# The first two output units of an RWKV layer as fp32 products of raw weights, most of them placed between the hops of the last chain

## The chip, the core and the metric

One core of one Trainium2 chip runs the whole program in one launch. The metric is device time in microseconds (us). Engines are named as the profile names them: PE (TensorE matmuls), PEld (its weight loads), DVE (VectorE), ACT (ScalarE), POOL (GpSimd), SP (SyncE, which issues the DMA transfers). L1564 is line 1564 of the kernel.

## What is computed

Two layers over 512 latent tokens and a prefix of 256 context tokens, width 1024. Layer 0 is grouped-query attention, layer 1 a bidirectional RWKV-7 mixer; behind each mixer stands a squared-ReLU MLP. The change is at the end of the layer 1 mixer, whose result for the latent tokens is

```python
def rwkv_out(y, r, k_dir, v, g, r_k, ln_w, ln_b, w_out):
    mean = jnp.mean(y, axis=-1, keepdims=True)
    var = jnp.mean(jnp.square(y - mean), axis=-1, keepdims=True)
    yn = ((y - mean) * lax.rsqrt(var + RWKV_GN_EPS)).reshape(B, T, H * N) * ln_w + ln_b
    rk = jnp.sum((r[None] * k_dir).reshape(2, B, T, H, N) * r_k, axis=(0, -1))[..., None]
    yn = yn + (rk * v.reshape(B, T, H, N)).reshape(B, T, H * N)
    return (yn.astype(v.dtype) * g) @ w_out

x = x + mod_x[2] * y_x
x = x + mod_x[5] * sq_relu_mlp(modulate(rms_norm(x, n2), mod_x[3], mod_x[4]), w_up, w_down)
```

`y` is the output of the scan, `g` the gate, and `@ w_out` a product of 512 x 1024 by 1024 x 1024.

## The kernel before

Activations lie transposed: partitions are 128 rows of the width, 8 row blocks k = 0 to 7, tokens run along the free axis. Large products are cut into **units** of 256 output columns. A unit is 8 row blocks by 2 tiles of 128 outputs. To keep fp32 accuracy at the fast rate each operand is split into a high part and a rest of type fp32r (weights: RAW into WH by ACT, then WL = RAW - WH by POOL or DVE; activations: AH and AL), and three products are summed: WH by AH, WL by AH, WH by AL. Two buffers s = 0, 1 alternate. Units are numbered through the program: `U_OUT1` = 56 to 59 are the four of `l1_w_out`, `U_MLP1` = 60 the first of the MLP. `pe_unit` does a whole unit with 512 tokens (48 matmuls, L393); the last two output units run in halves of 256 tokens by `pe_before_norm` (`pe_part`, L571, 48 matmuls a half), so that the norm of the first 256 tokens can begin under the second half.

The scan runs by pairs of heads (8 groups g) and directions (d), so NQ = 16 chains q. `slots` interleaves in a fixed order the preparation of chain s, the inverses of chain s-1 and the hops of chain s-2; in the last slot only chain 15 is left. A chain has 12 **hops**, one per block of 64 tokens; each is a loop between PE and DVE: AR by state (L1564), DVE RH (L1664), XIF by RH (L1576), DVE VSA (L1670), VSA by BKT (L1585), DVE state SS (L1677), next hop. From hop 4 on there is also the output: SS by AR (L1573) behind RH and VSA by MT (L1590) behind VSA. The last of these ends `y` and raises `y_done`. Then, for an odd chain, comes the group norm: PE sums over a head (L1597, L1600), gate (L1603), variance (L1606); on DVE YC copy, centring (L1690), and at the end two scalings, the gate and the write of the gated rows: tokens 0 to 255 to `X[:, g, 0:256]`, 256 to 511 to `OG[:, g]` (L1707, L1708), which raises `og_ready`; on ACT the square (L1634), Ln and Exp (L1639, L1641). The gated rows of groups 0 to 6 lie there since the chains before. In the last group norm ACT and DVE also split the gated rows (`out_high`, `out_low`) between these steps.

SP loads unit 56 once the last preparation is through (`lv_ready`), unit 57 only when the last gated row is written (`og_ready` of KT + 2). RAW, WH and WL share their memory with tiles of the scan.

Of the kernel before, what the change touches and what calls it, by code (L numbers as in the profile page):

```python
# [19 lines left out]
ALU = mybir.AluOpType  # L20
ACT = mybir.ActivationFunctionType
# [98 lines left out]
LANDED = [sum(2 if v in FOUR else 1 for v in range(u % 2, u + 1, 2)) for u in range(UNITS)]  # L120


def build(nc, a, out):

    stack = ExitStack()
    with stack:
# [202 lines left out]
        f_read = sem("final_read")  # L329

# [1215 lines left out]

        def pe_chain(e, q):
# [7 lines left out]
            for j, c in enumerate(ORDER[d]):
# [32 lines left out]
                if j >= NCH - NX:  # L1588
                    for h, k in enumerate(HEADS):
                        mm = e.matmul(bank(7)[k, out_cols], VSA[gp][:, c, k], mt(b, 2 * m + h, 2 + cp), start=False,  # L1590
                                      stop=(d == 1), skip_group_check=True)
                    if j == NCH - 1 and d == 1:
                        mm.then_inc(y_done, 1)
                yield
            if d == 1:
# [24 lines left out]
        def act_chain(e, q):  # L1620
            g, d = divmod(q, 2)
            if q == NQ - 1:
                act_split(e, U_OUT1, 0, LANDED[U_OUT1])
            for _ in range(3 * NCH):
                yield
            if d == 1:
                yield
# [18 lines left out]
        def dve_chain(e, q):  # L1646
# [35 lines left out]
            if d == 1:  # L1682
# [9 lines left out]
                if g == KT - 1:  # L1692
                    out_low(e, range(4))
# [20 lines left out]
        def _(sp):  # L1714
# [31 lines left out]
            for i in range(4):  # L1746
# [4 lines left out]
                         a["table"][:, OFFSET["rope_cos"][0]:OFFSET["rope_cos"][0] + 2 * TX]).then_inc(ld_rope, 16)  # L1751
# [78 lines left out]
            for s in range(2):  # L1830
                load_unit(sp, U_OUT1 + 2 + s, s, plain(a["l1_w_out"], UC * (2 + s), s))
# [16 lines left out]
        def _(pool):  # L1848
# [8 lines left out]
            pool.wait_ge(ld_rope, 16)  # L1857
# [30 lines left out]
            for u in range(U_OUT1, U_MLP1):  # L1888
                pool_split(pool, u, u % 2)
# [5 lines left out]
        def _(act):  # L1895
# [320 lines left out]
        def _(dve):  # L2216
# [158 lines left out]
```

## Time and profile before

| | us |
|---|---|
| median of 3 runs (2527.04 to 2534.26) | 2531.09 |
| the profiled execution's own time | 2524.67 |
| its span in the profile | 2522.9 |
| PE busy | 2304.2 (91%) |
| DVE busy | 1102.3 (44%) |
| ACT busy | 917.4 (36%) |
| POOL busy | 677.5 (27%) |

The profile is one execution; 1.8 us of its time lie outside the span. Busy time counts a matmul from its start to the modelled end of its data, so records overlap: in a packed row of 512-column fp32r matmuls each lasts 0.39 us and the next starts 0.23 us after it. What a matmul costs PE is read from start to start. An fp32 matmul leaves two records, each with a weight load. PEclk is the share of full clock that was granted, 1.00 at 2.4 GHz and 0.50 at 1.2 GHz.

### The profile page before, as it was taken

The page shows a single profiled execution, that of the slowest core. Times are in us where ns is not written, and L with a number is a line of the kernel's source. Part 1 is how long each engine was busy: PE and PEld are TensorE (multiplying, and loading weights), DVE is VectorE, ACT ScalarE, POOL GpSimd, SP SyncE. Part 2 cuts the span into 40 slices and gives each one's busy share as a digit, 9 for nine tenths or more (in the row PEclk, how much of TensorE's full clock was granted, in tenths as well). Part 3 has the DMA queues.
Part 4 walks back from the last instruction along what each step waited for, and adds up shares of the span by engine and source line. Part 5 has one row for each costly group of instructions (what it writes and reads, how often), then busy time and mean ns, then how long its engine had stood idle before and what let it go on. Part 6 is the DMA issues. An engine that isn't in the chain of part 4 may idle for free.

```text
span 2522.9 us, 65240 instructions
## 1 busy us (share of the span) xinstructions
PE 2304.2 (91%) x27579; PEld 1907.5 (76%) x27579; DVE 1102.3 (44%) x2424; ACT 917.4 (36%) x1630; POOL 677.5 (27%) x487
## 2 busy tenths in 40 slices
PE   5998899899999999999968888898888868999998
PEld 3776677788888888878737777777777757888887
DVE  2327666351111212562346666676666644411213
ACT  3555555342121212542224334334334314422324
POOL 0334555213233323123211211211211202344442
PEclk9999999999999999999989999999999978999998
DMA  8124555112221222123400000000000002233321
GB/s 247 51 50 156 180 169 166 51 51 67 67 67 50 66 67 67 51 88 117 149 5 23 13 21 16 12 23 15 23 12 14 20 2 84 84 100 100 100 91 60
DMA packets 172316, 176.37 MB, mean 70 GB/s; under 512 B 26512, under 2 KB 160032, under 8 KB 172064
## 3 DMA queue, kind: packets, MB, share of 16 engines
q1 hardware_dynamic: 172064, 172.62, 21.8%
q8 instruction: 206, 3.38, 0.6%
q14 instruction: 46, 0.38, 0.0%
HBM read 161.06 MB, written 11.53 MB: 68 GB/s over the span
## 4 chain that ended last, share of the span: by engine, by line
PE 81%; DVE 8%; issue 5%; ACT 4%; DMA 1%; POOL 1%; SPq 0%; ACTq 0%; DVEq 0%; PEldq 0%
PE PS L393 38%; PE PS L1474 5%; PE PS L571 4%; PE PS L413 3%; PE PS L767 2%; PE PS L1585 2%; PE PS L1459 2%; PE PS L1280 2%; PE PS L748 2%; PE PS L1449 2%; PE PS L727 1%; PE PS L1564 1%; PE PS L757 1%; PE PS L1134 1%; PE PS L1576 1%
## 5 line engine op out<-in xcount | busy, mean ns | idle before, releaser
L373 POOL TENSOR_TENSOR WL<-RAW,WH 128x1024 fp32r<-128x1024 f32 x168 | 402.9, 2420 | 992.7 <-ACT WH L354 992.7
L393 PE MATMUL PS<-AH,WH 128*128 128x512 f32 (+1 forms) x1024 | 363.9, 355 | 8.2 <-POOL WL L373 4.4
L393 PE MATMUL PS<-AH,WL 128*128 128x512 f32 (+1 forms) x1024 | 364.2, 356 | 0.0
L393 PE MATMUL PS<-AL,WH 128*128 128x512 f32 (+1 forms) x1024 | 361.5, 353 | 0.0
L354 ACT ACTIVATE WH<-RAW 128x1024 fp32r<-128x1024 f32 x168 | 167.9, 1047 | 277.6 <-PE PS L393 265.7
L393 PE MATMUL PS<-BH,WL 128*128 128x512 f32 (+1 forms) x672 | 239.2, 356 | 0.0
L393 PE MATMUL PS<-BH,WH 128*128 128x512 f32 (+1 forms) x672 | 238.5, 355 | 0.0
L393 PE MATMUL PS<-BL,WH 128*128 128x512 f32 (+1 forms) x672 | 237.6, 354 | 0.0
L393 PEld LDWEIGHTS PS<-AH,WH 128*128 128x128 f32 x1024 | 193.6, 189 | 38.9 <-POOL WL L373 5.4
L393 PEld LDWEIGHTS PS<-AL,WH 128*128 128x128 f32 x1024 | 192.9, 188 | 28.5
L393 PEld LDWEIGHTS PS<-AH,WL 128*128 128x128 f32 x1024 | 193.3, 189 | 26.7 <-issue 0.2
L690 DVE SCALAR_TENSOR_TENSOR X<-PS,MOD,X 128x256 f32 (+3 forms) x96 | 57.6, 656 | 356.4 <-PE PS L393 356.4
L666 DVE TENSOR_TENSOR HSQ<-HRL 128x768 f32<-128x768 f32 (+1 forms) x64 | 51.8, 851 | 317.8 <-ACT HRL L654 317.8
L1459 PE MATMUL PS<-XIT,AR 64*64 64x64 f32 x3840 | 162.4, 226 | 22.9 <-issue 22.7
L1436 POOL TENSOR_TENSOR MT<-MT,CT 128x256 f32<-128x256 f32 x48 | 39.2, 817 | 512.9 <-DVE MT L1418 512.9
L1474 PE MATMUL PS<-XI,MT 64*64 64x64 f32 x3840 | 165.7, 223 | 5.1 <-issue 3.1
L869 POOL TENSOR_TENSOR PB<-PB,SMS 128x768 f32<-128x768 f32 (+1 forms) x96 | 123.9, 1301 | 124.5 <-DVE SMS L891 124.1
L1474 PEld LDWEIGHTS PS<-XI,MT 64*64 64x64 f32 x3840 | 138.0, 135 | 19.5 <-issue 14.2
L1459 PEld LDWEIGHTS PS<-XIT,AR 64*64 64x64 f32 x3840 | 128.4, 134 | 31.5 <-issue 30.5
L1449 PE MATMUL PS<-AR,XIT 64*64 64x64 f32 x3072 | 137.8, 223 | 12.3 <-issue 8.5
L1507 ACT ACTIVATE XI<-PS 128x128 f32<-128x128 f32 x192 | 53.5, 279 | 256.2 <-PE PS L1459 255.9
L654 ACT ACTIVATE HRL<-PS 128x768 f32<-128x768 f32 (+1 forms) x64 | 41.7, 704 | 274.0 <-PE PS L393 262.6
(262 smaller groups left out, 4966.7 us busy)
## 6 DMA issues: line engine op xcount, KB each, us to landing
ADW<-l_ada_w SPq DMA_DIRECT2D x40, 1024.0 KB, 5.4
RAW<-l_mlp_up SPq DMA_DIRECT2D x64, 512.0 KB, 4.2
RAW<-l_mlp_down SPq DMA_DIRECT2D x64, 512.0 KB, 4.3
RAW<-l_w_rkv SPq DMA_DIRECT2D x24, 512.0 KB, 4.9
rwkv_scratch<-STG SPq DMA_DIRECT2D x24, 384.0 KB, 3.4
ADA<-l_ada_w SPq DMA_DIRECT2D x4, 2048.0 KB, 15.6
RAW<-l_w_in SPq DMA_DIRECT2D x16, 256.0 KB, 5.3
RAW<-l_w_out SPq DMA_DIRECT2D x16, 256.0 KB, 5.4
```

Source lines behind the costliest of these rows:

```text
L354: e.activation(WH[:, s, rows], RAW[:, s, rows], ACT.Copy).then_inc(w_high[h], 1)
L373: e.tensor_tensor(WL[:, s, rows], RAW[:, s, rows], WH[:, s, rows], ALU.subtract).then_inc(w_split[h], 1)
L393: mm = e.matmul(dst, w[:, s, k, n * P:(n + 1) * P], r[:, k, lo:hi], start=(k == 0 and i == 0), stop=(k == KT - 1 and i == 2), skip_group_c ...
L413: mm = e.matmul(dst, w[:, s, k, n * P:(n + 1) * P], r[:, k, lo:hi], start=(k == 0 and i == 0), stop=(k == KT - 1 and i == 2), skip_group_c ...
L571: mm = e.matmul(tile_ps(4 * s + 2 * n)[:, at:at + hi - lo], w[:, s, k, n * P:(n + 1) * P], r[:, k, lo:hi], start=(k == 0 and x == 0), stop ...
L666: e.tensor_tensor(HSQ[:, n, lo:], HRL[:, n, lo:], HRL[:, n, lo:], ALU.mult).then_inc(h_sq, 1)
L690: ins = e.scalar_tensor_tensor(out=x, in0=tile_ps(4 * s + 2 * n)[:, a0:a1], scalar=gate, in1=x, op0=ALU.mult, op1=ALU.add)
L869: e.tensor_tensor(p, p, SMS[:, rs:rs + 1].to_broadcast([P, span(m) * P]), ALU.mult).then_inc(p_scaled, 1)
L1449: return e.matmul(bank(1)[t, i * C:(i + 1) * C], XIT[o, 4 * (v % 3) + i, :], UM[v % 2][o, i, :], start=True, stop=True, skip_group_check=True)
L1459: return e.matmul(out, UM[v % 2][o, i, :], XIT[o, 4 * (v % 3) + i, :], start=True, stop=True, skip_group_check=True)
L1474: mm = e.matmul(bank(0)[o, i * C:(i + 1) * C], mt(b, u, 0)[t], XI[t, u, :] if n >= 3 else IDN[t, t], start=True, stop=True, skip_group_che ...
L1507: e.activation(every_other(XI[:, four, :], v // 3, q % 2), every_other(bank(1)[:, 0:256].rearrange("p (u t) -> p u t", u=4), v // 3, q % 2 ...
```

## The change

Units 56 and 57 are no longer split. They are computed by `direct`, which multiplies the raw fp32 weights by the fp32 gated rows themselves: for each row block k, tile n and token half one matmul of 128 x 128 by 256 columns, 64 in all (32 a unit), in place of 96 of 512 columns. Of the 56 that need only row blocks 0 to 6, 35 are issued in the last chain, one behind each group of PE's hop matmuls, 3 between the matmuls of the group norm, and 18 behind them. The remaining 8 (row block 7) wait for `og_ready`.

- The raw weights: unit 56 into RAW buffer 0, unit 57 into a new place RAW_SECOND, both loaded at `lv_ready`. Unit 58 goes to RAW_THIRD, loaded when group 6 is gated; unit 59 to RAW buffer 1, loaded at `y_done`.
- ACT's split in the last chain, and POOL's behind it, are now those of unit 58. Unit 59 is split behind the last Exp, its low halves by DVE behind the additions of units 56 and 57.
- `out_high` of blocks 0 to 2 comes ahead of the last chain, 3 to 6 behind `y_done`. `out_low` of 0 to 6 stands behind the centring.
- Behind the last square ACT has a one-column Ln, with its table load, ahead of the wait for the variance.
- The first additions read banks of `direct_bank`. DVE's squares of the norm stand behind both additions.
- A semaphore is freed: the rope table's load counts on `ld_const`.

```diff
+DIRECT = (U_OUT1, U_OUT1 + 1)
...
+        RAW_SECOND = place("RAW_SECOND", 120.25, [P, KT, UC])
+        RAW_THIRD = place("RAW_THIRD", 71, [P, KT, UC])
+        DIRECT_RAW = (RAW[:, 0], RAW_SECOND[:, :, :])
...
+        def direct_bank(j, n):
+            return bank(2 * n + 1 + j)
+
+        def direct(e, j, i):
+            k, n, half = i // 4, i // 2 % 2, i % 2
+            if i == 0:
+                e.wait_ge(direct_landed, 64)
+            elif k == KT - 1:
+                e.wait_ge(og_ready, KT + 2)
+            rows = OG[:, k, :] if half else X[:, k, 0:TX // 2]
+            return e.matmul(direct_bank(j, n)[:, half * (TX // 2):(half + 1) * (TX // 2)], DIRECT_RAW[j][:, k, n * P:(n + 1) * P],
+                            rows, start=(k == 0 and half == 0), stop=(k == KT - 1), skip_group_check=True)
+
+        EARLY = 4 * (KT - 1)
+
+        def direct_early(e, first, count):
+            for i in range(first, first + count):
+                direct(e, *divmod(i, EARLY))
...
             for j, c in enumerate(ORDER[d]):
...
                     mm.then_inc(rhs_done, 1)
+                if last:
+                    direct_early(e, 3 * j, 1)
                 yield
...
                 mm.then_inc(sa_done, 1)
+                if last:
+                    direct_early(e, 3 * j + 1, 1)
                 yield
...
+                if last and j < NCH - 1:
+                    direct_early(e, 3 * j + 2, 1)
                 yield
...
                 e.matmul(bank(5), HEAD1, YC[:, :], start=True, stop=True).then_inc(gn_mean, 1)
+                if last:
+                    direct_early(e, 3 * NCH - 1, 2)
                 yield
...
                 e.matmul(bank(6), G2G[gp][:, :], LG[:, :], start=True, stop=True).then_inc(gn_gate, 1)
+                if last:
+                    direct_early(e, 3 * NCH + 1, 1)
...
                 if g == KT - 1:
-                    out_high(e, range(4, 6))
+                    e.activation(LNW[:, :], EPSC[:, 0:1], ACT.Ln)
...
             sp.wait_ge(lv_ready, NQ)
-            load_unit(sp, U_OUT1, 0, plain(a["l1_w_out"], 0, 0))
-            sp.wait_ge(og_ready, KT + 2)
-            load_unit(sp, U_OUT1 + 1, 1, plain(a["l1_w_out"], UC, 1))
...
+            out1 = w_view(a["l1_w_out"])
+            for j in range(2):
+                for h in range(2):
+                    rows = slice(4 * h, 4 * h + 4)
+                    sp.dma_start(DIRECT_RAW[j][:, rows, :], out1[:, rows, bass.ds(UC * j, UC)]).then_inc(direct_landed, 16)
...
+            direct_early(pe, 3 * NCH + 2, 2 * EARLY - 3 * NCH - 2)
             for j in range(2):
-                pe_unit(pe, U_OUT1 + j, j, AH, AL, streams=(1,), k_ready=og_split)
+                for i in range(EARLY, EARLY + 4):
+                    mm = direct(pe, j, i)
+                mm.then_inc(w_used, 1)
             pe_before_norm(pe, 3, U_OUT1 + 2, AH, AL, og_split)
...
-            out_low(dve, range(4, KT))
+            out_low(dve, range(KT - 1, KT))
             for j in range(2):
-                add_dve(dve, U_OUT1 + j, j % 2, 2 * j, 1, 2, TC, (3, j))
+                dve.wait_ge(w_used, U_OUT1 + j + 3)
+                for n in range(2):
+                    dve.scalar_tensor_tensor(out=X[:, 2 * j + n, TC:], in0=direct_bank(j, n),
+                                             scalar=MOD[:, 1, 16 + 2 * j + n, 0:1], in1=X[:, 2 * j + n, TC:],
+                                             op0=ALU.mult, op1=ALU.add).then_inc(evac_dve if n else x_done, 1)
+                dve.wait_ge(w_split[j], U_OUT1 + 5)
+                low_half(dve, U_OUT1 + 3, 1, j)
```

Line numbers in the orders below are those of each kernel. PE at the end of the last chain, before: the last hop's state, SA and output steps, then the group norm's four matmuls and at once the units.

```order
8670 L1585 MATMUL PS<-VSA,BKT 64x64 x2
8671 L1590 MATMUL PS<-MT,VSA 64x64 x2
8672 L1564 MATMUL PS<-SS,AR 64x64 x2
8673 L1573 MATMUL PS<-AR,SS 64x64 x2
8674 L1576 MATMUL PS<-RH,XIF 64x64 x2
8675 L1590 MATMUL PS<-MT,VSA 64x64 x2
8676 L1597 MATMUL PS<-YT,CK 128x512
8677 L1600 MATMUL PS<-YC,CK 128x512
8678 L1603 MATMUL PS<-LG,G2G 128x512
8679 L1606 MATMUL PS<-YQ,CK 128x512
8680 L393 MATMUL PS<-AH,WH 128x512
8681 L393 MATMUL PS<-AH,WL 128x512
```

Between two groups of a hop PE has nothing to issue.

The same place now; X and OG are the gated rows, RAW_SECOND the weights of unit 57.

```order
8704 L1564 MATMUL PS<-X,RAW_SECOND 128x256
8705 L1594 MATMUL PS<-SS,AR 64x64 x2
8706 L1564 MATMUL PS<-OG,RAW_SECOND 128x256
8707 L1605 MATMUL PS<-AR,SS 64x64 x2
8708 L1608 MATMUL PS<-RH,XIF 64x64 x2
8709 L1564 MATMUL PS<-X,RAW_SECOND 128x256
8710 L1624 MATMUL PS<-MT,VSA 64x64 x2
8711 L1633 MATMUL PS<-YT,CK 128x512
8712 L1636 MATMUL PS<-YC,CK 128x512
8713 L1564 MATMUL PS<-OG,RAW_SECOND 128x256
8714 L1564 MATMUL PS<-X,RAW_SECOND 128x256
8715 L1641 MATMUL PS<-LG,G2G 128x512
```

A product stands behind each group of the hop, two stand between mean and gate.

PE behind the group norm now (before, the row behind the variance is the first of the 96 unit matmuls, as above). Rows with RAW are the last row block of unit 56, the last with RAW_SECOND that of unit 57, L576 is unit 58.

```order
8735 L1564 MATMUL PS<-OG,RAW_SECOND 128x256
8736 L1564 MATMUL PS<-X,RAW 128x256
8737 L1564 MATMUL PS<-OG,RAW 128x256
8738 L1564 MATMUL PS<-X,RAW 128x256
8739 L1564 MATMUL PS<-OG,RAW 128x256
8740 L1564 MATMUL PS<-X,RAW_SECOND 128x256
8741 L1564 MATMUL PS<-OG,RAW_SECOND 128x256
8742 L1564 MATMUL PS<-X,RAW_SECOND 128x256
8743 L1564 MATMUL PS<-OG,RAW_SECOND 128x256
8744 L576 MATMUL PS<-AH,WH 128x256
8745 L576 MATMUL PS<-AH,WL 128x256
8746 L576 MATMUL PS<-AL,WH 128x256
```

The last products are eight of 256 columns, and unit 58 follows directly.

ACT in the last group norm before: YQ<-YC is the square, the table loads are those of Ln and Exp.

```order
1128 L1611 ACTIVATE AH<-OG 128x256
1129 L1610 ACTIVATE AH<-X 128x256
1130 L1611 ACTIVATE AH<-OG 128x256
1131 L1634 ACTIVATE YQ<-YC 128x512
1132 L1610 ACTIVATE AH<-X 128x256
1133 L1611 ACTIVATE AH<-OG 128x256
1134 L1610 ACTIVATE AH<-X 128x256
1135 L1611 ACTIVATE AH<-OG 128x256
1136 L1639 ACT_TABLE_LOAD
1137 L1639 ACTIVATE YQ<-PS,EPSC 128x512
1138 L1641 ACT_TABLE_LOAD
1139 L1641 ACTIVATE YQ<-YQ 128x512
```

Two blocks are split between the square and the first table load.

The same place now.

```order
1134 L1651 ACTIVATE AH<-OG 128x256
1135 L1650 ACTIVATE AH<-X 128x256
1136 L1651 ACTIVATE AH<-OG 128x256
1137 L1681 ACTIVATE YQ<-YC 128x512
1138 L1683 ACT_TABLE_LOAD
1139 L1683 ACTIVATE LNW<-EPSC 128x1
1140 L1686 ACTIVATE YQ<-PS,EPSC 128x512
1141 L1688 ACT_TABLE_LOAD
1142 L1688 ACTIVATE YQ<-YQ 128x512
1143 L2057 ACTIVATE WH<-RAW 128x1024 x2
```

The Ln table load moved from behind two blocks of splitting and the wait for the variance to directly behind the square, and the split of unit 59 (WH<-RAW) stands behind Exp.

## Rows read from the trace of the kernel before

**Rows 1.** Page, section 4: engines on the chain that ended last.
```profile
PE 81%; DVE 8%; issue 5%; ACT 4%; DMA 1%; POOL 1%; SPq 0%; ACTq 0%; DVEq 0%; PEldq 0%
```

**Rows 2.** Windows: busy of PE, PEld, DVE, ACT, POOL; PEclk, DMA share, GB/s.
```profile
2050.00:2056.00 6.00, 4.30 (x113) 3.25 (x108) 3.12 (x10) 3.27 (x7) 1.13 (x1) 1.00 0.01 3
2056.00:2088.00 32.00, 18.62 (x189) 13.62 (x190) 11.13 (x43) 0.15 (x1) 3.51 (x2) 0.50 0.01 1
2088.00:2094.00 6.00, 6.00 (x9) 2.22 (x9) 3.67 (x9) 4.12 (x13) 0.00 (x0) 0.53 0.00 0
```

**Rows 3.** Timeline (start, duration, instruction, [idle <-releaser]), last chain, first hops.
```profile
2053.92 0.33 PE L1576 MATMUL PS<-LV,XIF 64*64 64x64 f32 x4 [0.16 <-ACT XIF L1514]
...
2054.72 0.39 PE L1585 MATMUL PS<-VSA,BKT 128*64 128x64 f32 x4 [0.47 <-DVE VSA L1670]
...
2055.58 0.33 PE L1564 MATMUL PS<-SS,AR 64*64 64x64 f32 x4 [0.47 <-DVE SS L1680]
...
2056.09 1.18 DVE L1667 TENSOR_SCALAR SW<-SS,WP 128x64 f32<-128x64 f32 x1
...
2056.32 0.48 PE L1576 MATMUL PS<-RH,XIF 64*64 64x64 f32 x4 [0.41 <-DVE RH L1664]
```

**Rows 4.** Same timeline, one plain hop: starts of neighbouring first steps.
```profile
2058.68 0.48 PE L1564 MATMUL PS<-SS,AR 64*64 64x64 f32 x4 [0.47 <-DVE SS L1677]
...
2061.47 0.48 PE L1564 MATMUL PS<-SS,AR 64*64 64x64 f32 x4 [0.47 <-DVE SS L1677]
```

**Rows 5.** Same timeline, hops with an output step, six hops apart.
```profile
2066.29 0.48 PE L1585 MATMUL PS<-VSA,BKT 128*64 128x64 f32 x4 [0.48 <-DVE VSA L1670]
...
2084.31 0.48 PE L1585 MATMUL PS<-VSA,BKT 128*64 128x64 f32 x4 [0.48 <-DVE VSA L1670]
```

**Rows 6.** Timeline of an earlier slot, full clock, neighbours without a wait.
```profile
1438.00 0.34 PE L1590 MATMUL PS<-MT,VSA 128*64 128x64 f32 x4
...
1438.26 0.46 PE L1459 MATMUL PS<-XIT,AR 64*64 64x64 f32 x16
...
1438.65 0.30 PEld L1597 LDWEIGHTS PS<-YT,CK 128*128 128x128 f32 x2
...
1439.62 1.02 PE L1600 MATMUL PS<-YC,CK 128*128 128x512 f32 x2
...
1440.57 0.67 PE L1280 MATMUL PS<-AR,KB 64*64 64x128 f32 x16
...
1452.66 1.56 PE L1221 MATMUL PS<-LA,A2X 128*128 128x256 f32 x4
```

**Rows 7.** Chain that ended last (start, duration, what), 2087 to 2101 us.
```profile
2087.33 0.48 PE PS L1590 x4
...
2089.82 1.72 PE PS L1600 x2
...
2092.29 0.63 ACT YQ L1634
...
2094.17 1.28 ACT L1639
...
2097.46 0.64 ACT YQ L1641
...
2100.13 0.34 DVE OG L1708
```

**Rows 8.** Timeline, PE: start of the second unit, start of the third.
```profile
2110.45 0.58 PE L393 MATMUL PS<-AH,WH 128*128 128x512 f32 x1 [3.45 <-POOL WL L373]
...
2123.08 0.28 PE L571 MATMUL PS<-AH,WH 128*128 128x256 f32 x1
```

**Rows 9.** Timeline, DVE: addition of a unit, low half of a unit.
```profile
2107.03 1.41 DVE L690 SCALAR_TENSOR_TENSOR X<-PS,MOD,X 128x512 f32<-128x512 f32 x2 [3.90 <-PE PS L393]
...
2152.73 1.21 DVE L367 TENSOR_TENSOR WL<-RAW,WH 128x1024 fp32r<-128x1024 f32 x1
```

**Rows 10.** Timeline, SP: loads of the output weights.
```profile
2013.69 100.49 SPq L341 DMA_DIRECT2D RAW<-l_w_out  x8
```

More of the change, by code:

```diff
@@ L119 @@
 FOUR = (0, 1, 2, 3, 6, 7, 8, 9, 54)
-LANDED = [sum(2 if v in FOUR else 1 for v in range(u % 2, u + 1, 2)) for u in range(UNITS)]
+DIRECT = (U_OUT1, U_OUT1 + 1)
+LANDED = [sum(2 if v in FOUR else 0 if v in DIRECT else 1 for v in range(u % 2, u + 1, 2)) for u in range(UNITS)]
 def build(nc, a, out):
@@ L608, in build, with act_around_norm @@
         SPLIT_AT = {1: (6, 7), 3: (1, 4)}
-        def act_around_norm(e, i, u, layer, half):
-            act_split(e, u - 1, 1, LANDED[u - 1])
+        def act_around_norm(e, i, u, layer, half, split=True):
+            if split:
+                act_split(e, u - 1, 1, LANDED[u - 1])
             e.sem_inc(evac_act, 1)
@@ L1553, in pe_chain @@
                 e.wait_ge(gn_sum, g + 1)
+            last = q == NQ - 1
+            if last:
+                e.wait_ge(lv_ready, NQ)
             e.nop(nofuse=True)
@@ L1603, in pe_chain @@
                 e.matmul(bank(6), G2G[gp][:, :], LG[:, :], start=True, stop=True).then_inc(gn_gate, 1)
+                if last:
+                    direct_early(e, 3 * NCH + 1, 1)
                 yield
@@ L1622, in act_chain @@
             if q == NQ - 1:
-                act_split(e, U_OUT1, 0, LANDED[U_OUT1])
+                for h in range(2):
+                    e.sem_inc(w_high[h], 2)
+                e.wait_ge(raw_landed[0], 32 * LANDED[U_OUT1 + 2])
+                for h in range(2):
+                    rows = slice(4 * h, 4 * h + 4)
+                    e.activation(WH[:, 0, rows], RAW_THIRD[:, rows, :], ACT.Copy).then_inc(w_high[h], 1)
+                e.wait_ge(og_ready, KT + 1)
+                e.wait_ge(gn_rk, KT)
+                out_high(e, range(3))
             for _ in range(3 * NCH):
@@ L1692, in dve_chain @@
                 if g == KT - 1:
-                    out_low(e, range(4))
+                    out_low(e, range(KT - 1))
                 yield
@@ L1826, in _ @@
             sp.wait_ge(lv_ready, NQ)
-            load_unit(sp, U_OUT1, 0, plain(a["l1_w_out"], 0, 0))
-            sp.wait_ge(og_ready, KT + 2)
-            load_unit(sp, U_OUT1 + 1, 1, plain(a["l1_w_out"], UC, 1))
-            for s in range(2):
-                load_unit(sp, U_OUT1 + 2 + s, s, plain(a["l1_w_out"], UC * (2 + s), s))
+            out1 = w_view(a["l1_w_out"])
+            for j in range(2):
+                for h in range(2):
+                    rows = slice(4 * h, 4 * h + 4)
+                    sp.dma_start(DIRECT_RAW[j][:, rows, :], out1[:, rows, bass.ds(UC * j, UC)]).then_inc(direct_landed, 16)
+            sp.wait_ge(og_ready, KT + 1)
+            for h in range(2):
+                rows = slice(4 * h, 4 * h + 4)
+                sp.dma_start(RAW_THIRD[:, rows, :], out1[:, rows, bass.ds(UC * 2, UC)]).then_inc(raw_landed[0], 16)
+            sp.wait_ge(y_done, KT)
+            for dst, src in plain(a["l1_w_out"], UC * 3, 1):
+                sp.dma_start(dst, src).then_inc(raw_landed[1], 16)
+            sp.wait_ge(w_used, U_OUT1 + 3)
             with sp.Fori(0, 4) as c:
@@ L1887, in _ @@
             slots(pool, pool_pre, pool_inverse, pool_chain)
-            for u in range(U_OUT1, U_MLP1):
-                pool_split(pool, u, u % 2)
+            for h in range(2):
+                pool.sem_inc(w_split[h], 2)
+            for h in range(2):
+                rows = slice(4 * h, 4 * h + 4)
+                pool.wait_ge(w_high[h], U_OUT1 + 3)
+                pool.tensor_tensor(WL[:, 0, rows], RAW_THIRD[:, rows, :], WH[:, 0, rows], ALU.subtract).then_inc(w_split[h], 1)
             with pool.Fori(U_MLP1 // 2 + 1, UNITS // 2) as i:
@@ L1994, in _ @@
             slots(act, act_pre, act_inverse, act_chain)
-            out_high(act, range(6, KT - 1))
+            act.wait_ge(raw_landed[1], 32 * LANDED[U_OUT1 + 3])
+            for h in range(2):
+                rows = slice(4 * h, 4 * h + 4)
+                act.activation(WH[:, 1, rows], RAW[:, 1, rows], ACT.Copy).then_inc(w_high[h], 1)
             act.wait_ge(og_ready, KT + 2)
@@ L2313, in _ @@
             slots(dve, dve_pre, dve_inverse, dve_chain)
-            out_low(dve, range(4, KT))
+            out_low(dve, range(KT - 1, KT))
             for j in range(2):
-                add_dve(dve, U_OUT1 + j, j % 2, 2 * j, 1, 2, TC, (3, j))
+                dve.wait_ge(w_used, U_OUT1 + j + 3)
[5 more added lines that the diff above has]
+                low_half(dve, U_OUT1 + 3, 1, j)
+            for j in range(2):
+                norm_dve_squares(dve, 3, j, 0)
             dve_around_norm(dve, 3, U_MLP1, 1, 1, 2)
```

16 lines of the change are left out of this document (8 added, 8 removed).

## The prediction

> **What bounds the kernel now.** I read the page first: the chain that ended last lies on PE for 81% [rows 1], so a change counts where PE waits or works off rate. The change touches one stretch, from the last chain to the first half of unit 58, so I read that in windows, then its timeline, then the chain through it. The reader is to see three things.
>
> In the last chain PE and DVE only take turns. The clock granted to PE is 1.00 up to 2056 us and 0.50 for the 32 us behind it [rows 2]: PE went from packed slots to small groups with waits. At full clock a link, from one PE group to the next, took 0.80 us (SA to state), 0.86 (state to next AR by SS), 0.74 (AR by SS to SA) [rows 3], so a plain hop would be 2.40. At half clock it takes 2.79 [rows 4], and a hop with output steps 3.00 (six of them in 18.02) [rows 5]. One hop lies beside POOL's split: a DVE multiply takes 1.18 us there [rows 3], and from 2055.58 to 2058.68 it is 3.10 us [rows 3, 4].
>
> In the group norm the chain goes through PE's sums at half clock (1.72 us for 512 fp32 columns), the square, then two blocks of ACT splitting before the Ln table load at 2094.17, to the gated rows at 2100.47 [rows 7]. That is 13.1 us behind the last output step at 2087.33, which I call Y.
>
> Behind it unit 57 starts only at 2110.45, after a wait of 3.45 us for its low half, and cold [rows 8]; its load was issued only at the gated rows. Unit 58 starts at 2123.08 [rows 8], Y + 35.75.
>
> **The change, term by term.** Everything is reckoned to the start of unit 58, the first work that is the same before and after.
>
> *Price of a product.* One of 256 and one of 512 fp32 columns last 1.56 us together at full clock; 512 columns with the handover to the next group of small ones take 0.95 from start to start [rows 6]. With 0.85 for 512, 0.43 for 256 and some 0.27 of drain both rows come out (0.43 + 0.85 + 0.27 = 1.55), and the handover from a full product to small matmuls is 0.10. The handover the other way, from a group of four records to what comes next, is 0.26 [rows 6].
>
> *35 products in the chain.* A link with a product needs PE for 0.26 + 0.43 + 0.10 = 0.79 us; with two groups (an output step beside SA or state) 0.12 more: the two extra groups add 3.00 - 2.79 = 0.21 to a hop now, 0.10 each [rows 4, 5], and I round up, since they no longer lie under a wait: 0.91. Each link is the longer of that and the present link at the clock granted. PE would then stream for 0.43 + 0.1 of about 0.8 us instead of 0.1, more than in the packed slot ahead of it, which kept 1.00; I take full clock throughout. A plain hop becomes 0.79 + 0.80 + 0.86 = 2.45, one with output 0.79 + 0.91 + 0.91 = 2.61. The chain from 2053.92: hop 0 has two links, 1.66; hops 1 to 3 7.35; 4 to 10 18.27; hop 11 1.70; POOL's collision, which stays since POOL splits unit 58 at the same place, 0.6. Sum 29.6 against 33.41 now (Y - 2053.92): **-3.8 us**. Bounds: with products that cost nothing, 2.40 a hop and 0.12 for its output steps, -4.7; with half the handovers on top, 0.18 a link over 34 links, +2.3.
>
> *Group norm, to Y' + 5.* At full clock, from the new last output step Y': rowsum from 0.26, mean from about 1.17 behind DVE's copy to 2.02, two products to 2.88, gate to 3.73, one product to 4.16, variance to 5.0. The square ends 1.38 behind the mean's data (2091.54 to 2092.92), near 3.6, so variance waits 0.5 us for PE, not for ACT. The Ln load (1.28) lies under that. From the end of that load to the end of Exp it is 2.65 now (2095.45 to 2098.10) and from there to the gated rows 2.37 [rows 7], so they come at 5.2 + 2.65 + 2.37 = Y' + 10.2 instead of Y + 13.1. This gain counts for nothing by itself, because PE is later.
>
> *18 products and 8.* PE has 18 x 0.43 = 7.7 us to do from 5.0 and comes to 12.75, 2.5 us behind the gated rows: it never waits for them. The eight of row block 7 take 3.4, to 16.2. Unit 58 also needs the banks of unit 56 read: its last product ends at 14.5, DVE adds it in 1.41 [rows 9], 16.1. Unit 58 starts at Y' + 16.35 instead of Y + 35.75: **-19.4 us**. In place of 96 matmuls of 512 columns, the wait of 3.45 us and a cold start there are 26 products; the other 38 lie in the chain and the norm. Cover that could go: DVE splits seven blocks between centring and Exp instead of four; if they ran over, the gated rows have 2.5 us of slack.
>
> *Moved splits.* ACT copies unit 59 in the 2.4 us between Exp and the gated rows, and nobody asks for it before 16. DVE has, from 14.7, two additions of 1.41 and two low halves of 1.21 [rows 9], ending at 20. Unit 59 asks for them at about 22: unit 57 takes 12.6 us for 48 matmuls of 512 columns with a cold start [rows 8], the half of unit 58 has 48 of 256, some 5.8. The norm squares follow and end near 23 to 24, so the first half of unit 58 is added about 1 us late; unit 59's first half, on which the norm chain hangs, ends at 27.9. Cost 0, with 3 us of cover; gone, each microsecond over it counts whole.
>
> *Loads.* Now 3 MB instead of 1 are asked for at 2013.69 [rows 10] and behind it, 40 us ahead of the first product. Unit 59 is asked for at Y' and read by ACT at Y' + 8; load, copy and low half together take 10 us now, from the gated rows to PE's start [rows 7, 8], so the load alone is there. Cost 0. The MLP's first loads come earlier in relation to the norm. The semaphore edit costs nothing.
>
> *Sum.* 2524.67 - 3.8 - 19.4 = 2501.5 us for the profiled execution. It lies 6.4 under the median of 2531.09, so against the median **2508 us** (-0.9%).
>
> **A rule weighed.** Rows 6 show small and full-array matmuls in a row at 0.10 and 0.26 us of handover, so the next weights load under the running product. The Trainium skill (TensorE: Matmul & The Clock Gate, Part 3, The mechanism) says that a weight load overlaps matmuls in flight only when its row group differs; a 128-row product has all of them. By the rule the loads come on top; by the rows they do not. What it would give is the first rival.
>
> **Rivals.**
> 1. *Weight loads exposed.* The two loads of a product cover 0.30 us in the trace [rows 6]. Added to 0.79 and 0.91 they make links of 1.09 and 1.21: 1.66 becomes 2.18, hops 3.27 and 3.63, last 2.3, sum 2.2 + 9.8 + 25.4 + 2.3 + 0.6 = 40.3, that is +6.9 in place of -3.8, and 18 + 8 products that follow each other stay packed. 2519 us. For it: the alternation of small and full is in every link; against it: rows 6.
> 2. *The clock falls all the same.* Cold, a link is 0.48 + 0.86 + 0.1 = 1.4 (a whole group [rows 4], then half of the 1.72 of 512 columns [rows 7]), 1.6 with output. Cold throughout from hop 2 gives 48 us of chain, +15, and some 3 in the norm: about 2529. Cold for half of it 2518. Against it: PE would be over 0.9 busy, and in the norm the clock rose at about 2093.6 after 6 us of such work [rows 2].
> 3. *DVE turns the gain back.* If its squares and additions run into unit 59's end by 2 to 4 us beyond the cover, 2510 to 2512. It cannot be told from the forecast by time, only by PE's wait in unit 58's second half.
> 4. *Slower.* Each alternation drains PE: a group's whole 0.48 us [rows 4], a load of 0.3, 0.86 cold, and 0.3 to drain and load again make 1.95 a link against 0.98 now (33.41 / 34), +33 us against -19.4: 2545. It decides from 0.57 us added to a link on. Rows 6 speak against it.
> 5. *The change does not do what it says*, because the raw weights or unit 59 land late. With 40 us of lead this is left at 1 in 100.
>
> **How the numbers follow.** Chances: forecast 0.62, rival 1 0.13, rival 2 0.12 (most of it the half-cold case), rival 3 0.08, rival 4 0.04, the rest 0.01. The forecast's own range, from the two bounds of the chain (-0.9 and +6.1 beside its term) and the 4 us by which the runs of before lie apart from their median, is 2502 to 2518. Range for 8 in 10, which takes in rival 1 and the milder cold cases: 2502 to 2521. A change under 0.3% (7.6 us) is about what a measurement of this kernel cannot tell from none. Faster by more than that, under 2523.5: all of the forecast, rivals 1 and 3 and the milder part of 2, 0.91. Within it 0.05, slower 0.04.
>
> **What the new profile would show.** Right: PEclk 1.00 from the chain's start on; hops of 2.4 to 2.7 us with output steps; product records behind each group; no PE wait between the variance and unit 58, which starts 16 to 17 us behind the last output step; Ln table load directly behind the square; PE's load of unit 60 and the norm behind as before. Wrong: links of 1.1 us and more with PE busy and full clock (rival 1), PEclk 0.50 in the hops (rival 2), PE waiting for RS or X in the second half of unit 58 (rival 3).

## The result and the profile after

| | before | changed |
|---|---|---|
| median of 4 runs each (us) | 2530.0 (2527.04 to 2534.26) | 2514.35 (2509.28 to 2515.45) |
| ratio | | 0.9933, 95% interval 0.9921 to 0.9945 |
| profiled execution (us) | 2524.67 | 2513.49 |

0.67% of 2530 us is 17 us, 14 to 20 by the interval. The forecast was 2508 in a range of 2502 to 2521: the gain is there, some 6 us smaller than forecast. The profiled execution, forecast at 2501.5, took 2513.49.

Two windows of the changed kernel follow: the last chain, then the stretch from the last output step (now L1624; its start is called Y') to the start of unit 58. Columns as in [rows 2].

```profile
2062.80:2095.80 33.00, 32.99 (x271) 19.03 (x271) 10.84 (x45) 3.59 (x8) 4.67 (x2) 1.00 0.01 2
2095.46:2111.93 16.47, 16.47 (x71) 12.60 (x71) 11.45 (x26) 10.74 (x20) 0.00 (x0) 1.00 0.20 64
```

In [rows 2] TensorE was busy for 18.62 of 32 us at a granted clock of 0.50; now it is busy all the time at 1.00. So it waits for nobody, and every microsecond here is TensorE's own. Its timeline shows that for one plain hop, here with the weight loads (PEld) of the first product:

```profile
2067.88 0.33 PE L1594 MATMUL PS<-SS,AR 64*64 64x64 f32 x4
2068.14 0.30 PEld L1564 LDWEIGHTS PS<-X,RAW 128*128 128x128 f32 x2
2068.14 0.70 PE L1564 MATMUL PS<-X,RAW 128*128 128x256 f32 x2
...
2068.77 0.33 PE L1608 MATMUL PS<-RH,XIF 64*64 64x64 f32 x4
...
2069.03 0.70 PE L1564 MATMUL PS<-OG,RAW 128*128 128x256 f32 x2
...
2069.66 0.28 PE L1619 MATMUL PS<-VSA,BKT 128*64 128x64 f32 x2
```

A group of small ones holds TensorE for 0.26 us (2067.88 to 2068.14), a product for 0.63 (2068.14 to 2068.77, again 2069.03 to 2069.66): a link is 0.89. That answers to [rows 4]; no row has a bracket with a wait any more. The two ends of the chain and hops with an output step, six of them between the second and third row from below:

```profile
2062.81 0.67 PE L1564 MATMUL PS<-X,RAW 128*128 128x256 f32 x2 [0.16 <-ACT XIF L1520]
2063.41 0.33 PE L1608 MATMUL PS<-LV,XIF 64*64 64x64 f32 x4
2064.30 0.34 PE L1619 MATMUL PS<-VSA,BKT 128*64 128x64 f32 x4
...
2072.33 0.34 PE L1619 MATMUL PS<-VSA,BKT 128*64 128x64 f32 x4
2075.12 0.34 PE L1619 MATMUL PS<-VSA,BKT 128*64 128x64 f32 x4
...
2092.55 0.34 PE L1619 MATMUL PS<-VSA,BKT 128*64 128x64 f32 x4
...
2095.46 0.34 PE L1624 MATMUL PS<-MT,VSA 128*64 128x64 f32 x4
```

Plain hops take 8.03 / 3 = 2.68 us, hops with an output step 17.43 / 6 = 2.90. From the first state product (2063.41) to Y' (2095.46) it is 32.05 us, with the product ahead of it 32.65; it was 33.41. **The chain gained 0.8 us**.

Behind it, ACT and DVE in the norm, then TensorE at unit 58:

```profile
2098.48 0.63 ACT L1681 ACTIVATE YQ<-YC 128x512 f32<-128x512 f32 x1
2099.13 1.28 ACT L1683 ACT_TABLE_LOAD   x1
...
2105.34 0.41 DVE L1755 TENSOR_TENSOR OG<-PS,YC 128x256 f32<-128x256 f32 x1
...
2110.26 1.41 DVE L2383 SCALAR_TENSOR_TENSOR X<-PS,MOD,X 128x512 f32<-128x512 f32 x2 [2.96 <-PE PS L1564]
2111.59 1.22 DVE L372 TENSOR_TENSOR WL<-RAW,WH 128x1024 fp32r<-128x1024 f32 x1
...
2111.93 0.35 PE L576 MATMUL PS<-AH,WH 128*128 128x256 f32 x1
...
2125.06 1.28 ACT L490 ACT_TABLE_LOAD   x1
```

The gated rows are ready at 2105.75, Y' + 10.3, and unit 58 starts at 2111.93, **Y' + 16.47**, where [rows 7, 8] had Y + 35.75: 19.3 us less. The Ln table of the norm behind is loaded 13.13 us past the start of unit 58; before it was 13.16 (2136.24 against 2123.08), so nothing is given back there. The stretch as a whole is 20.0 us shorter in this pair of profiles. Yet the profiled executions differ by 11.2 only, because the changed one comes to the last chain 8.9 us later: ACT's copy that starts it runs at 2062.29, at 2053.39 before. The lag is there already where the first output weights are asked for (2022.83 us against 2013.69), and ahead of that the change touches nothing but the semaphore of the rope tables.

So two things were open. Does the change itself cost time upstream, and is the shortened stretch worth 17 us or 20? And what in it brings the gain?

### The profile page after: what moved, and what is told of

It is laid out like the page before. It is cut to its first block, busy times and chain, and to the rows that moved or that the text cites. A ratio compares the mean times of both kernels' runs of the same rounds, so it can differ in the third digit from the quotient of the medians.

```text
span 2511.7 us, 65288 instructions
## 1 busy us (share of the span) xinstructions
PE 2309.8 (92%) x27611; PEld 1909.1 (76%) x27611; DVE 1103.1 (44%) x2426; ACT 913.6 (36%) x1627; POOL 662.7 (26%) x481
## 4 chain that ended last, share of the span: by engine, by line
PE 82%; DVE 8%; issue 5%; ACT 4%; DMA 1%; POOL 1%; SPq 0%; ACTq 0%; DVEq 0%; PEldq 0%
PE PS L398 38%; PE PS L1480 5%; PE PS L576 4%; PE PS L418 3%; PE PS L773 2%; PE PS L1465 2%; PE PS L1286 2%; PE PS L1619 2%; PE PS L754 2%; PE PS L1455 2%; PE PS L733 1%; PE PS L1564 1%; PE PS L763 1%; PE PS L1140 1%; PE PS L1594 1%
## 5 line engine op out<-in xcount | busy, mean ns | idle before, releaser
L378 POOL TENSOR_TENSOR WL<-RAW,WH 128x1024 fp32r<-128x1024 f32 x160 | 383.5, 2419 | 953.7 <-ACT WH L359 953.7
L398 PE MATMUL PS<-AH,WH 128*128 128x256 f32 (+1 forms) x992 | 351.0, 354 | 3.1 <-DVE AL L2339 2.4
L398 PE MATMUL PS<-AH,WL 128*128 128x256 f32 (+1 forms) x992 | 351.6, 354 | 0.0
L398 PE MATMUL PS<-AL,WH 128*128 128x256 f32 (+1 forms) x992 | 348.9, 352 | 0.0
L359 ACT ACTIVATE WH<-RAW 128x1024 fp32r<-128x1024 f32 x160 | 159.9, 1047 | 271.8 <-PE PS L398 265.7
L398 PEld LDWEIGHTS PS<-AH,WH 128*128 128x128 f32 x992 | 187.7, 189 | 31.2 <-issue 2.6
L398 PEld LDWEIGHTS PS<-AL,WH 128*128 128x128 f32 x992 | 187.0, 189 | 27.2
L398 PEld LDWEIGHTS PS<-AH,WL 128*128 128x128 f32 x992 | 187.6, 189 | 25.3
L1465 PEld LDWEIGHTS PS<-XIT,AR 64*64 64x64 f32 x3840 | 129.0, 135 | 32.4 <-issue 31.3
```

What stands on the lines that cost most here:

```text
L359: e.activation(WH[:, s, rows], RAW[:, s, rows], ACT.Copy).then_inc(w_high[h], 1)
L378: e.tensor_tensor(WL[:, s, rows], RAW[:, s, rows], WH[:, s, rows], ALU.subtract).then_inc(w_split[h], 1)
L398: mm = e.matmul(dst, w[:, s, k, n * P:(n + 1) * P], r[:, k, lo:hi], start=(k == 0 and i == 0), stop=(k == KT - 1 and i == 2), skip_group_c ...
L1465: return e.matmul(out, UM[v % 2][o, i, :], XIT[o, 4 * (v % 3) + i, :], start=True, stop=True, skip_group_check=True)
```

## Experiments

Theory A: the gain is fp32 products put where TensorE had idled; TensorE bounds the whole stretch; the lag upstream is chance. Rival B: the lag is caused by the change. Rival C: the gain is the early loads and the missing split of unit 57. Each experiment ran in five rounds beside the kernel before. In the table "start" is the first state product of the last chain, "chain" from there to the last output step, "tail" from there to unit 58; a name such as "changed, all behind" means the changed kernel with that one edit.

| kernel | ratio (95%) | start | chain | tail |
|---|---|---|---|---|
| before | 1 | 2053.92 | 33.41 | 35.75 |
| changed | 0.9933 (0.9921, 0.9945) | 2063.41 | 32.05 | 16.47 |
| e1 before again | 1.0000 (0.9989, 1.0010) | 2058.64 | 33.42 | 32.36 |
| e2 before, rope semaphore | 0.9994 (0.9985, 1.0003) | 2062.17 | 33.42 | 35.49 |
| e3 changed, all behind | 0.9998 (0.9985, 1.0010) | 2053.33 | 33.22 | 34.37 |
| e4 changed, one a hop | 0.9994 (0.9985, 1.0003) | 2054.82 | 38.94 | 28.39 |
| e5 changed, own rope semaphore | 0.9923 (0.9904, 0.9942) | 2053.45 | 32.05 | 16.47 |
| e6 changed, no small Ln | 0.9933 (0.9913, 0.9954) | 2053.45 | 32.05 | 16.47 |
| e7 changed, four a hop | 0.9944 (0.9926, 0.9963) | 2049.19 | 38.26 | 14.05 |
| e8 before, unit 57 loaded early | 0.9989 (0.9978, 1.0001) | 2050.72 | 33.42 | 32.62 |
| e9 changed, two a hop | 0.9935 (0.9920, 0.9949) | 2048.75 | 30.71 | 21.65 |
| e10 changed, bunched | 0.9947 (0.9931, 0.9962) | 2051.71 | 38.49 | 16.47 |

In the kernels with a product ahead of the first state product (changed, e5, e6, e7) another 0.60 us belongs to the chain.

### e1: the kernel before a second time

No edit.

> The kernel before, unchanged, a second time. Both theories: ratio 1.000, within 0.998 to 1.002. Its profile is laid beside the first profile of the kernel before at the same instructions. If the upstream lag of 8.9 us that the changed kernel showed at the start of the last chain is chance, two profiles of this one kernel should lie apart by several us as well (3 to 8 us at the last chain, opening in jumps where the granted clock dips); if it is caused by the change, they should lie within 1 us of each other all the way.

The start lies 4.7 us later than in the first profile, in the very same program. And the tail is 3.4 us shorter. The timelines of ACT and TensorE in this profile; the second row answers to [rows 8]:

```profile
2109.86 2.01 ACT L354 ACTIVATE WH<-RAW 128x1024 fp32r<-128x1024 f32 x2 [4.26 <-DMA RAW<-l_w_out]
...
2113.40 0.50 PE L393 MATMUL PS<-AH,WH 128*128 128x512 f32 x1 [2.03 <-POOL WL L373]
```

The load of unit 57, asked for at 2100.49 in the first profile, was read by ACT 6.4 us later; here it took 5.0 (2104.87 to 2109.86). So the wait was 2.03 instead of 3.45 us, and the clock held: the windows behind it show 1.00 here and 0.69 in the first profile.

```profile
2114.06:2119.56 5.50, 5.50 (x26) 4.54 (x25) 2.20 (x1) 2.01 (x2) 5.50 (x3) 1.00 0.50 166
```

```profile
2109.33:2114.83 5.50, 4.38 (x12) 3.48 (x13) 0.89 (x1) 2.52 (x4) 5.50 (x3) 0.69 0.05 14
```

(First e1, then the kernel before, each from the stretch in which unit 57 starts or just has.) Of the 3.4 us, 0.35 lies ahead of the load, which e1 asks for 12.81 us behind the last output step and the first profile 13.16; 1.4 is the wait itself, and 1.6 the work of unit 57 behind it (11.02 us to unit 58 in e1, 12.63 in the first profile, where part of it ran at the lower clock). e2's profile repeats the first one's: a wait of 3.51 us, a clock of 0.50 from 2120 to 2122 us, a tail of 35.49. The kernel before thus has a tail of two lengths in these three profiles, 35.6 and 32.4, and by the first profile or by e1's the change is worth 19.3 or 15.9 us there.

### e2: the rope semaphore alone

```diff
-  ...2 * TX]).then_inc(ld_rope, 16)
+  ...2 * TX]).then_inc(ld_const, 16)
-  pool.wait_ge(ld_rope, 16)
+  pool.wait_ge(ld_const, 32)
...
-  dve.wait_ge(ld_rope, 16)
+  dve.wait_ge(ld_const, 32)
```

> The kernel before with one edit of the change alone: the rope tables count on the constants' semaphore instead of one of their own. Theory A (the upstream lag is chance): ratio 1.000, within 0.999 to 1.001. Rival B (this edit costs the first 0.3 us and sets the clock's phases against the work, and so makes the lag): ratio 1.0015, 3 to 4 us slower.

0.9994 with an upper bound of 1.0003, where B wanted 1.0015: rival B has no support from this edit. The profile starts the chain at 2062.17, as late as the changed kernel, while the kernel's time is that of before; a single profile's start says nothing of the kernel.

### e3: all 56 early products behind the variance

```diff
-  direct_early(e, 3 * j, 1)           # and the other four calls in pe_chain
...
-  direct_early(pe, 3 * NCH + 2, 2 * EARLY - 3 * NCH - 2)
+  direct_early(pe, 0, 2 * EARLY)
```

> The changed kernel with no product between the hops or in the norm: all 56 early products run behind the variance's group, and loads, banks and everything else stay. Theory A (the gain is products put where TensorE would idle): the chain goes back to half clock and 33.4 us (+0.8 beside the changed kernel), 38 more products stand behind the variance at 0.43 us each (+16.3), and the first of them run at a lower clock (0 to +2), so 17 to 19 us over the changed kernel and ratio 0.999 to the kernel before (0.9975 to 1.001). Rival C (the gain is mostly the early loads and the missing split of unit 57, which removed its wait of 3.45 us and more): clearly faster than the kernel before, ratio 0.996 or below.

0.9998: the whole gain is gone, although all loads, banks and splits of the change are in place. The chain is back at 33.2 us and half clock; TensorE's timeline shows one of its hops, 2.80 us long as in [rows 4], with the waits back:

```profile
2059.72 0.49 PE L1615 MATMUL PS<-VSA,BKT 128*64 128x64 f32 x4 [0.47 <-DVE VSA L1707]
...
2062.52 0.49 PE L1615 MATMUL PS<-VSA,BKT 128*64 128x64 f32 x4 [0.48 <-DVE VSA L1707]
```

The tail is 17.9 us longer than in the changed kernel (expected 16.3 to 18.3). Rival C falls: the early loads and the missing split are all there and do not make a faster kernel by themselves. A count fits this, though it was not tested by itself. A unit as split operands is 48 matmuls of 512 columns, 0.23 us apart (2099.24 to 2099.47 in the timeline of e1), so 11 us; two units are 22 us. The 64 products take 64 x 0.43 = 27.5 us for both. In fp32 the two units thus cost TensorE some 5.5 us more when packed, which is about what the missing waits give.

### e8: the early load alone

```diff
   load_unit(sp, U_OUT1, 0, plain(a["l1_w_out"], 0, 0))
-  sp.wait_ge(og_ready, KT + 2)
+  sp.wait_ge(y_done, KT)
   load_unit(sp, U_OUT1 + 1, 1, plain(a["l1_w_out"], UC, 1))
```

> The kernel before with one edit: the load of unit 57 is issued behind the last output step instead of behind the gated rows, about 13 us earlier; everything is still split. Tells how much of the gain is the early load alone. Expected: TensorE no longer waits for the low halves of unit 57 (2.0 to 3.5 us in the profiles so far) and the clock no longer falls behind that wait (1.7 us where it did), so 2 to 5 us off the kernel before, ratio 0.9985 (0.9980 to 0.9995). If the early load were most of the gain, the ratio would come near 0.994.

0.9989, with 1 still in the interval: a sixth of the gain, a third at the most by the interval. The tail of 32.62 is no shorter than e1's 32.36. The wait for unit 57 is gone, as expected, but another took its place. Timelines of POOL, DVE and TensorE:

```profile
2099.04 4.97 POOL L373 TENSOR_TENSOR WL<-RAW,WH 128x1024 fp32r<-128x1024 f32 x2 [42.74 <-ACT WH L354]
```

```profile
2098.85 0.41 DVE L1617 TENSOR_TENSOR AL<-OG,AH 128x256 fp32r<-128x256 f32 x1
2099.18 2.62 DVE L1616 TENSOR_TENSOR AL<-X,AH 128x256 fp32r<-128x256 f32 x1
2101.72 2.57 DVE L1617 TENSOR_TENSOR AL<-OG,AH 128x256 fp32r<-128x256 f32 x1
```

```profile
2104.35 0.50 PE L393 MATMUL PS<-AH,WH 128*128 128x512 f32 x1 [1.95 <-DVE AL L1617]
```

POOL's split now falls on the last two low halves of the gated rows. While it runs, each takes 2.6 us instead of 0.41, and TensorE waits 1.95 us for them. The change as made has no POOL work there at all: that is part of what it avoids.

### e5: the changed kernel with its own rope semaphore

```diff
+  direct_landed = ld_rope             # the rope load counts 16 on it, the direct loads 64
...
-  e.wait_ge(direct_landed, 64)
+  e.wait_ge(direct_landed, 80)
```

> The changed kernel with the rope tables on a semaphore of their own again (the direct loads then count on the same one, from 16 to 80). So far two profiles of the kernel before start the last chain 4.7 us apart, which speaks for chance. Theory A: the same ratio as the changed kernel, 0.993 to 0.995; the start of the last chain anywhere between 2053 and 2064 us; chain of 32.0 to 32.7 us and unit 58 at 16.5 us behind the last output step again. Rival B (the layout of semaphores makes the upstream lag): ratio 0.990 to 0.992 and a start near 2054.

0.9923, in whose interval the changed kernel's 0.9933 lies. The start is 2053.45; chain and tail repeat to 0.01 us. Over all twelve profiles the start wanders between 2048.75 and 2063.41, in both kinds of kernel. B is not needed for anything seen.

### e6: without the small Ln behind the square

```diff
   if g == KT - 1:
-      e.activation(LNW[:, :], EPSC[:, 0:1], ACT.Ln)
```

> The changed kernel without the small Ln behind the square, so that the table of Ln is loaded behind the variance. Theory A: the gated rows come about 0.5 to 1.3 us later (the table load of 1.28 us is no longer under the variance's group), TensorE has 18 products before it needs them and does not wait; unit 58 stays at 16.5 us behind the last output step; ratio to the kernel before 0.993 to 0.995. Rival (the gated rows set the end of the stretch): unit 58 1.3 us later and a wait of TensorE for OG.

The end is as theory A has it, but the expectation was wrong on the gated rows: they come at the same time as in e5, 10.3 us behind the last output step. ACT's timeline shows why:

```profile
2088.51 0.63 ACT L1681 ACTIVATE YQ<-YC 128x512 f32<-128x512 f32 x1
2089.16 1.28 ACT L1684 ACT_TABLE_LOAD   x1
2090.80 0.69 ACT L1684 ACTIVATE YQ<-PS,EPSC 128x512 f32<-128x512 f32 x1 [0.36 <-PE PS L1646]
```

The table load of the variance's own Ln starts directly behind the square, before the sum that this Ln waits for. The small Ln brings nothing. So in [rows 7] it was the splits standing between that made the load late, not the wait for the variance.

### e4, e9, e7: one, two and four products a hop

```diff
# e4: one, behind the state product L1608
-  direct_early(e, 3 * j, 1)
...
-  direct_early(e, 3 * j + 1, 1)
+  direct_early(e, j, 1)
# e9: that one as 2 * j, and 2 * j + 1 behind the state's step
# e7: 4 * j; 4 * j + 1 and 4 * j + 2 in a row behind the state product; 4 * j + 3
```

> The changed kernel with one product in each hop of the last chain (behind the state product) instead of three: 12 in the chain, 3 in the norm, 41 behind it. If one product a hop is enough to hold the full clock: links without a product take about 0.66 us, a hop 0.89 + 2 x 0.66 = 2.2 and the chain 27 us (-5.6 beside the changed kernel); 23 more products stand behind at 0.43 (+9.9); sum 4 us over the changed kernel, ratio 0.995. If the clock falls to half: hops of 3.2 us and a chain of 38 (+6), sum +16, ratio 0.9995. My guess is the first, at 6 in 10.

> The changed kernel with two products in each hop (behind the state product and behind the state's step): 23 in the chain, 3 in the norm, 30 behind it. With one product a hop the clock fell to half in the third hop; with three it held. If two hold it: a hop of about 0.89 + 0.89 + 0.78 = 2.56 us instead of 2.67, chain -1.3 and no first product ahead of it (-0.6), 12 more products behind at 0.43 (+5.2), sum +3.3 us over the changed kernel, ratio 0.9943. If the clock falls: hops of 4.1 us, chain +17, sum +22 and a ratio of 1.001. My guess is the first, at 7 in 10.

> The changed kernel with four products in each hop instead of three, two of them in a row behind the state product: 47 in the chain, 3 in the norm, 6 and then the 8 of the last rows behind it. Theory A (TensorE sets every link; in a run of products only one weight load lies open, at the first): the second product of a pair starts 0.43 to 0.53 us behind the first, the chain grows by 12 x 0.43 = 5.2 us; behind the variance 6 products end near 7.9 us past the last output step, and TensorE waits 2.4 us or so for the gated rows, which come at 10.3; unit 58 near 14.0 instead of 16.5; sum +2.7 us over the changed kernel, ratio 0.9943. Rival (a link still has slack, so a fourth product is partly hidden): chain +2 us or less and a sum below the changed kernel, ratio 0.992.

**One** gains nothing: 0.9994, which cannot be told from e3's 0.9998, and the longest chain of all. Windows of e4, in the chain's first hops and in those behind:

```profile
2055.00:2060.00 5.00, 3.07 (x28) 1.77 (x25) 2.55 (x8) 3.40 (x8) 4.31 (x2) 1.00 0.00 0
2060.00:2093.00 33.00, 26.40 (x191) 16.60 (x192) 9.14 (x37) 0.00 (x0) 0.35 (x1) 0.51 0.01 1
```

The clock falls as before, and at half clock a product adds 0.6 us to each hop (3.6 with an output step against 3.0 in [rows 5]). The guess at 6 in 10 was the wrong one; the other branch, a chain of 38 us and 0.9995, came true. Chain 38.9 and tail 28.4 give 18.2 us over the changed kernel by the profile, 15 by the ratios.

**Two** hold the clock. Window and timeline of e9:

```profile
2050.00:2079.00 29.00, 24.21 (x232) 14.60 (x232) 10.97 (x43) 2.33 (x7) 4.28 (x2) 1.00 0.01 1
```

```profile
2066.70 0.33 PE L1594 MATMUL PS<-SS,AR 64*64 64x64 f32 x4
2067.45 0.27 PE L1603 MATMUL PS<-AR,SS 64*64 64x64 f32 x2 [0.42 <-DVE RH L1709]
```

The link without a product takes 0.75 (2066.70 to 2067.45), as in [rows 3]; the chain is 1.3 us shorter, the tail 5.2 longer, both as worked out. By the profile this is 3.2 us worse than three; the ratios, 0.9935 and 0.9933, cannot tell them apart.

**Four**: TensorE's timeline in e7, a link with a pair, and its end of the tail.

```profile
2059.55 0.33 PE L1608 MATMUL PS<-RH,XIF 64*64 64x64 f32 x4
2059.81 0.70 PE L1564 MATMUL PS<-OG,RAW 128*128 128x256 f32 x2
2060.35 0.59 PE L1564 MATMUL PS<-X,RAW 128*128 128x256 f32 x2
2060.87 0.34 PE L1619 MATMUL PS<-VSA,BKT 128*64 128x64 f32 x4
...
2097.80 0.70 PE L1564 MATMUL PS<-X,RAW 128*128 128x256 f32 x2 [2.49 <-DVE OG L1755]
```

The pair takes 0.54 + 0.52 = 1.06, one alone 0.63: the second costs its full 0.43, nothing of it is hidden. So a link with one product has no slack left. The chain grew by 6.2 us, 12 x 0.43 and 1.0 more where the second hop waits 0.96 for DVE beside POOL's split; the wait for the gated rows and 14.05 are as expected.

### e10: the three products of a hop in a row

```diff
-  direct_early(e, 3 * j, 1)
...
-  direct_early(e, 3 * j + 1, 1)
+  direct_early(e, 3 * j, 3 if j < NCH - 1 else 2)
...
-  direct_early(e, 3 * j + 2, 1)
```

> The changed kernel with the same 35 products in the chain, but the three of a hop in a row behind the state product. Theory A (what is hidden is the wait of one link for VectorE, so that a product pays only where there is one): the long link takes 0.26 + 0.54 + 0.43 + 0.52 = 1.75 us, the other two about 0.85 and 0.74 without a product, a hop 3.3 instead of 2.67 us and the chain +7 to +8; nothing changes behind it; ratio 0.9960. Rival (what counts is only how much work stands in a hop, by the clock): no change, ratio 0.993.

```profile
2068.71 0.70 PE L1564 MATMUL PS<-OG,RAW 128*128 128x256 f32 x2
2069.25 0.59 PE L1564 MATMUL PS<-X,RAW 128*128 128x256 f32 x2
2069.68 0.59 PE L1564 MATMUL PS<-OG,RAW 128*128 128x256 f32 x2
2070.21 0.34 PE L1617 MATMUL PS<-VSA,BKT 128*64 128x64 f32 x4
...
2071.02 0.33 PE L1594 MATMUL PS<-SS,AR 64*64 64x64 f32 x4 [0.36 <-DVE SS L1720]
```

The chain is 6.4 us longer with the same products (5.8 with the one that no longer stands ahead), and waits of 0.36 and 0.41 are back in the other two links. By the profile A is right that the place counts, if somewhat over in size (7 to 8 expected). The ratio, 0.9947, is a loss of 3.5 us against the changed kernel's 0.9933, but its lower bound of 0.9931 hardly excludes the rival's 0.993: the profile decides here, not the ratio.

## Why the prediction was right, and which term was off

**Sign and mechanism** held: the clock stays at 1.00 from the chain's start, the products lie behind every group, TensorE never waits between the variance and unit 58. e3 shows that the products' place is what brings the gain.

**"Group norm", "18 products and 8", "Moved splits", "Loads"** held: gated rows at 10.3 (10.2 forecast), unit 58 at 16.47 (16.35), DVE done with the low halves of unit 59 at 19.8 (20), no cost behind. The bound I feared, DVE running over (rival 3), did not appear. That the Ln load "directly behind the square" comes from the small Ln was wrong in reason, not in time (e6).

**The term "35 products in the chain" was mis-sized**: -3.8 forecast, -0.8 measured. Without collision and first product I had 29.0 us, measured 32.05: 3.05 over, 0.09 for each of 34 links. The product ahead of the first state product, which my sum left out, adds 0.60; POOL's collision, 0.6 in the sum, did not show in this kernel. The 0.09 is in "Price of a product". Start to start, a product in a packed run costs 0.43, as forecast. One between small groups costs 0.63, where I had 0.43 + 0.10. e7 and e10 split it up: the first of a run stands 0.54 ahead of the second, the second of three 0.43 ahead of the third, the last 0.52 or 0.53 ahead of the small group. So there is 0.1 at the run's start and 0.1 at its end, and I had priced the end alone. [Rows 6] had held it: from the first product of 512 columns, whose loads stand at 1438.65, to the second at 1439.62 it is 0.97 us, not 0.85. And 256 and 512 columns last 1.56, which is 0.43 + 0.85 + 0.28; I called all the 0.28 drain, though the second product's record of 1.02 leaves only 0.17 for it.

That the 0.1 at the start is a weight load lying open is argued, not shown. For it speak the loads' rows in the changed kernel. In the packed run, the 18 products behind the variance, the two loads of a product begin 0.2 us ahead of it, under its forerunner:

```profile
2102.08 0.41 PEld L1564 LDWEIGHTS PS<-X,RAW_SECOND 128*128 128x128 f32 x2
2102.29 0.59 PE L1564 MATMUL PS<-X,RAW_SECOND 128*128 128x256 f32 x2
...
2102.72 0.59 PE L1564 MATMUL PS<-OG,RAW_SECOND 128*128 128x256 f32 x2
```

In the hop (2068.14 above) both start with the product. If that reading holds, rival 1 was right in kind for a third of its 0.30. The rule of the Trainium skill (TensorE: Matmul & The Clock Gate, Part 3, The mechanism), that a weight load overlaps matmuls in flight only when its row group differs, does not agree with the packed rows here: two full-array loads, 0.41 us together, lie there under full-array products that come 0.43 apart. The same section of the Trainium skill also has loads pulled ahead when they go to a background weight buffer; the packed rows would fit that, and no run here tests it.

**Rival 2** did not come at three products a hop; at one it did (e4), and there it cost all the gain. **Rival 1's sum** has a slip: its 3.63 for a hop with output counts the output step in all three links, where the forecast has it in two. With 1.09 + 1.21 + 1.21 = 3.51 its chain is 39.5 instead of 40.3 and its time 2518 instead of 2519; it stays inside the stated range.

**The sum against the median**: I set the whole difference against one profile of before, which had the long tail. The three profiles in which this stretch is as before (before, e1, e2) have tails of 35.75, 32.36 and 35.49, mean 34.5. Against that the stretch gains 18.1 + 0.8 = 18.9 us, and 17 (14 to 20) was measured. So of the forecast's 23.2 us, 3.0 are the mis-sized chain and 1.3 the tail, nearly all of it the long tail of the one profile that I set it against; what is left of the difference lies within the interval. In the pair of profiled executions the miss is 12.0 us: the 3.0 of the chain, 0.1 of the tail and the lag of 8.9 us upstream. The forecast had no term for that lag. Starts 4.7 us apart in two profiles of one program, and 10 us apart in the changed kernel and e5, with ratios alike, show that it varies from one execution to the next. Why the start wanders was not tried.

## What to carry to other kernels

Where an engine idles in a chain of hand-offs and loses its clock by it, independent work between the hand-offs can come for nothing. Here 38 products, 16.3 us of packed work, went into chain and norm; against e3 that gained 18.5 us by the profiles and 16 by the ratios. But it took enough work at every hop, spread over the links: one product a hop lost all the gain, three in a row cost a third of it by the profile. How much of the gain is the held clock and how much the hidden work was not separated. Price filler work by its start-to-start time when it stands singly between other work, not by that of a packed run. And profile the kernel before twice: a wait that hangs on a transfer's landing had two lengths here, 1.4 us apart, and what followed made 3.0 of it.

## Unexpected of the hardware

- An fp32 product of 256 columns costs 0.43 us in a run of its like and 0.63 between groups of small ones, both at full clock.
- A table load on ACT (1.28 us) starts ahead of the wait of the activation that needs it: in e6 it starts at 2089.16, while the activation waits for its sum and starts at 2090.80.
- While POOL subtracts two SBUF tiles, a DVE subtraction of two SBUF tiles takes 2.6 instead of 0.41 us. The Trainium skill (SBUF — State Buffer, Who interferes with whom) says that a DVE instruction with two SBUF inputs contends with a GpSimd instruction that reads SBUF; e8 agrees.
- A transfer that landed 1.4 us later cost 3.0 us (kernel before against e1): the wait was 3.45 instead of 2.03 us, and behind the longer one the clock stood at 0.69 in the window of 5.5 us, behind the shorter one at 1.00, which goes with 1.6 us more for the same unit.
